# Moving the low weight buffers of three weight streams by 128 bytes in SBUF

## What is computed

```python
h = rms_norm(x)
q, kc, vc, ks, vs, kw, vw, gn, u, v, ga, gb = split(h @ w_in)          # 1024 x 4376
o_a = nsa_attention(q, ...)            # compressed + selected + window branches
o_b = u * gmlp_spatial(v)
x += (sigmoid(ga) * (o_a @ w_branch_a) + sigmoid(gb) * (o_b @ w_branch_b)) @ w_out
x += cross_attention(rms_norm(x) @ w_cq, memory) @ w_co
h = rms_norm(x)
x += (silu(h @ w_gate) * (h @ w_up)) @ w_down                           # 1024 x 2816, 2816 x 1024
y = rms_norm(x)
```

## Time and profile before

| | |
|---|---|
| device time, median of 3 runs | 2215.38 us (2214.71 to 2215.53) |
| the profiled execution | span 2214.8 us from the first to the last instruction |
| TensorE matmul busy | 2118.7 us, 96% |
| VectorE / GpSimd / ScalarE busy | 929.5 / 611.8 / 551.1 us |
| mean share of the DMA engines | 22.7% of their time for the largest queue |
| mean granted TensorE clock | 0.983 of 2.4 GHz |

### The profile page before, as it was taken

One profiled execution on the slowest core, in us unless ns is written; L12 is line 12 of the kernel. 1 busy time (PEld: TensorE's weight loads), 2 busy tenths in 40 slices (PEclk: granted clock), 3 DMA queues, 4 the chain that ended last, 5 costly groups with the idle time before them and its releaser, 6 DMA issues. The chain is left out here.

```text
span 2214.8 us, 38450 instructions
## 1 busy us (share of the span) xinstructions
PE 2118.7 (96%) x14076; PEld 1962.7 (89%) x14076; DVE 929.5 (42%) x1958; ACT 551.1 (25%) x1151; POOL 611.8 (28%) x531
## 2 busy tenths in 40 slices
PE   7999999988989999799999988999999999999998
PEld 6999999965855767599999878999999999999997
DVE  4111111186336676455661346563333333333335
ACT  5002211122326655222030332221111111111112
POOL 2233322245224444412212322212212122121220
PEclk9999999999979999899999999999999999999999
DMA  6212222394323000544212432110211112111121
GB/s 199 55 47 62 72 90 93 127 262 151 90 62 136 1 2 1 142 146 146 85 39 67 191 120 62 46 49 29 67 31 55 48 33 62 33 53 48 33 62 78
DMA packets 206648, 175.77 MB, mean 79 GB/s; under 512 B 25867, under 2 KB 186348, under 8 KB 205963
## 3 DMA queue, kind: packets, MB, share of 16 engines
q1 hardware_dynamic: 197450, 152.96, 22.7%
q10 hardware_dynamic: 4448, 11.81, 1.5%
q0 software_dynamic: 4640, 9.61, 1.5%
HBM read 147.02 MB, written 27.39 MB: 79 GB/s over the span
## 5 line engine op out<-in xcount | busy, mean ns | idle before, releaser
L152 POOL TENSOR_TENSOR tail_w_lo<-mem_last_slot,tail_w_hi 128x1024 fp32r<-128x1024 f32 (+1 forms) x94 | 183.3, 1950 | 689.8 <-ACT tail_w_hi L140 689.8
L191 PE MATMUL ff_psum<-tail_hi,tail_w_hi 128*128 128x352 f32 x1056 | 341.2, 323 | 1.0 <-PEq L2112 1.0
L192 PE MATMUL ff_psum<-tail_lo,tail_w_hi 128*128 128x352 f32 x1056 | 338.5, 321 | 0.0
L193 PE MATMUL ff_psum<-tail_hi,tail_w_lo 128*128 128x352 f32 x1056 | 338.2, 320 | 0.0
L191 PE MATMUL bank<-mix_hi,in_w_hi 128*128 128x352 f32 x840 | 271.9, 324 | 1.3 <-issue 1.3
L192 PE MATMUL bank<-mix_lo,in_w_hi 128*128 128x352 f32 x840 | 270.0, 321 | 0.0
L193 PE MATMUL bank<-mix_hi,in_w_lo 128*128 128x352 f32 x840 | 269.9, 321 | 0.0
L140 ACT CAST tail_w_hi<-mem_last_slot 128x1024 fp32r<-128x1024 f32 (+1 forms) x94 | 81.2, 863 | 509.3 <-PE ff_psum L193 433.4
L191 PEld LDWEIGHTS ff_psum<-tail_hi,tail_w_hi 128*128 128x128 f32 x1056 | 198.1, 188 | 2.0 <-issue 1.5
L192 PEld LDWEIGHTS ff_psum<-tail_lo,tail_w_hi 128*128 128x128 f32 x1056 | 198.4, 188 | 0.1
L193 PEld LDWEIGHTS ff_psum<-tail_hi,tail_w_lo 128*128 128x128 f32 x1056 | 197.9, 187 | 0.0
(11 more groups left out here) (394 smaller groups left out, 3822.2 us busy)
## 6 DMA issues: line engine op xcount, KB each, us to landing
in_raw<-w_in SPq DMA_DIRECT2D x70, 256.0 KB, 3.2
mem_last_slot<-w_gate SPq DMA_DIRECT2D x44, 256.0 KB, 3.2
mem_last_slot<-w_up SPq DMA_DIRECT2D x44, 256.0 KB, 3.3
mem_last_slot<-w_down SPq DMA_DIRECT2D x80, 128.0 KB, 2.2
gate_kept<-x_first ACTq DMA_DIRECT2D x16, 528.0 KB, 2.7
uv<-gate_kept SPq DMA_DIRECT2D x16, 528.0 KB, 4.6
mem_ring<-cache_mem_v SPq DMA_DIRECT2D x8, 1024.0 KB, 13.2
mem_ring<-cache_mem_k SPq DMA_DIRECT2D x7, 1024.0 KB, 7.0
```

What stands on the lines that cost most here:

```text
L152: pool.tensor_tensor(lo, raw, hi.bitcast(F32), ALU.subtract).then_inc(self.split, 1)
L191: pe.matmul(out, hi, x_hi, start=k == 0, stop=False)
L192: pe.matmul(out, hi, x_lo, start=False, stop=False)
L193: last = pe.matmul(out, lo, x_hi, start=False, stop=k == len(terms) - 1)
```

## The change

`place_halves` allocates each low buffer 256 bytes longer and uses its middle, so that the low weights start 128 bytes after the start of their allocation. Nothing else is edited.

```diff
+W_SHIFT = 32
 ...
     def place_halves(self, sb, ctx, name, depth, slots=(0, 1)):
         for s in slots:
             self.w_hi[s] = sb(ctx, f"{name}_w_hi{s}", [P, depth, P], F32R)
-            self.w_lo[s] = sb(ctx, f"{name}_w_lo{s}", [P, depth, P], F32R)
+            self.w_lo[s] = sb(ctx, f"{name}_w_lo{s}", [P, depth * P + 2 * W_SHIFT], F32R)[:, W_SHIFT:W_SHIFT + depth * P].rearrange("p (k c) -> p k c", k=depth)
```

## The result

| | before | changed |
|---|---|---|
| device time, median of 8 runs each | 2215.82 us | 2221.79 us (2219.78 to 2225.68) |
| ratio | | 1.0024, 95% interval 1.0014 to 1.0035 |
| span of the profiled execution | 2214.8 us | 2219.4 us |

The changed kernel is slower by 0.24%, some 5.3 us. That lies in the range, between the forecast (no change) and the slower rival, and just beyond the 0.2% that a measurement can tell. All ratios are of undisturbed executions: one of the kernel before (5344 us) and one of both128 (11060 us) lie far outside the others and are left out.

What follows compares the result with a forecast made beforehand. The prediction took TensorE's own products as the bound. Every part of the change was put at 0 us, so the profiled 2214.8 us plus 0.6 for the median gave 2215.4 us, with a range of 2204 to 2230.

Steps and rivals of the forecast that it cites:

- slower rival: Own streams' matmuls: each flip of relative place costs cycles; 14.7 us at full size (2230), put at 2227; chance 0.30.
- What bounds the kernel: TensorE, busy for 96% of the span; its weight products, 1501 us or 68%, are what the change can touch.
- No cost on GpSimd, ScalarE and SyncE: They handle the same sizes elsewhere; GpSimd has 689.8 us of waiting to cover a slower subtraction: 0 us.
- No cost of the moves by 256 and 512 bytes: High weights of slot 1 and activations of mid and tail keep their relative place modulo 256: 0 us.
- Only relative places count: TensorE's gaps follow where weights and activations start against each other modulo 256, not their absolute places; no size.
- The swap: Own streams, gap after line 192: 161.7 and 155.0 ns exchange between even and odd k + c; sum 0.
- The down projection: Low weights there: 1.4 ns to either side on 1440 matmuls, 2.0 us, taken as 0.
- The faster rival: Own streams: the low load under the second product is cheap in all steps; -8.9 us, 2206.5; chance 0.27.
- The far case: Own streams: all matmuls at the shortest averaged gap, 155.0 ns; -31.6 us, 2184; chance 0.03.
- The rule against any effect: TensorE has independent read ports for moving operand and weights and never waits, so the kernel stays at 2215.4 us.

Runs made afterwards that it cites:

- both128: Kernel before, with high and low weights of all streams both moved 128 bytes against the activations; measured ratio 0.9999.
- nolow: Changed kernel, with the third matmul of each step reading high weights in place of low ones; one run, 2217.3 beside 2217.4 us.
- low256: Kernel before, with low weights moved by 256 bytes against the high weights of slot 0, in place of 128; measured ratio 1.0000.
- align64: Kernel before, with 8 floats ahead of the big buffers on either side, so all start at multiples of 64 bytes; measured ratio 0.9987.
- actlow128: Kernel before, with the low activations of all streams starting 128 bytes later and weights as before; measured ratio 1.0097.
- high128: Kernel before, with the high weights moved by 128 bytes and the low weights kept in place modulo 256; measured ratio 1.0027.
- stride_in: Kernel before, with the weight blocks of a tile 640 bytes apart in place of 512, in the stream in alone; measured ratio 1.0029.
- both64: Kernel before, with high and low weights both moved 64 bytes against the activations; measured ratio 1.0045.
- both32: Kernel before, with high and low weights both moved 32 bytes against the activations; measured ratio 1.0068.

## Why the prediction was right or wrong

- **What bounds the kernel.** Right. The change is in the gaps of TensorE's weight products, on all dense own tiles, and the waits of the other engines didn't move.
- **No cost on GpSimd, ScalarE and SyncE.** Right, and shown by nolow: the writes to the new place are there and cost nothing.
- **No cost of the moves by 256 and 512 bytes.** Right, by low256.
- **Only relative places count.** Right as against absolute places, by low256 and align64, where buffers are elsewhere and own tiles take the same. But they are not all that counts: in actlow128 the same places gave 11.480 and 11.640 us.
- **The swap.** This is the step that failed. The prediction had the gap after line 192 follow the place of the block being loaded under it, and the two values 161.7 and 155.0 change places. They stayed: 161.7 and 155.8 after. Since both128 and high128 do exchange even and odd, and the change doesn't, the low block's own place doesn't choose between them; the high blocks' place does. The sum in a running chunk is nevertheless what the swap gave, 0, by another course: chunk 0 takes 3.813 before and after. The forecast of no change was lost on a term that the prediction put at nothing without naming it: what happens when a new chunk begins. Chunks 1 and 2 have some steps off the pattern there, before as well (the gaps of chunk 1 begin with 189, 194, 186 and 195, 192, 192 cycles). With low and high weights apart more steps are off, up to the fifth, and they are dearer, 0.047 us per tile in all, 5.2 us in the kernel. Which chunk starts are disturbed agrees with what the addresses say: k + c is odd in the last step of chunk 0 and again in the first of chunk 1, even in the last of chunk 1 and again in the first of chunk 2, and goes on alternating only from chunk 2 into chunk 0 of the next tile, the one chunk that begins in the pattern.
- **The size.** That the measured time lies in the range is in part luck: the range was wide enough for it only because it held the slower rival at full size. That rival's 11.3 to 14.7 us were twice to three times too much, and its mechanism is refuted: the place flips at each matmul in the steady part of the changed kernel, at no extra cost, and stride_in, without flips, is slower.
- **The down projection.** Its sum stayed within the 2 us allowed (0 in the steady tiles, 0.1 us in the first ones of the five groups), though single gaps changed there, too.
- **The faster rival** has nothing for it in any run: where the second product's gap was short in every step (chunk 1 of stride_in), the third's was longer, and no steady own tile was cheaper than before.
- **The far case.** The 149.2 ns that the prediction set beside it are, in the section of the Trainium skill that it names, the gap of an isolated matmul, and not that of a stream in which each matmul has a weight load of its own, as here. No tile came nearer to it than 158.98 ns per matmul.
- **The rule against any effect.** The Trainium skill, "SBUF — State Buffer", section "Who interferes with whom", has two independent read ports for TensorE and TensorE waiting on no one. On the waiting, nolow agrees: GpSimd's writes to the new place cost TensorE nothing. But own tiles took 11.447 to 11.667 us with the same instructions and the granted clock at 1.00, and it made a difference where weights lay against activations (both64, both32). So independent ports don't mean that places can't matter: for these float32r products they moved a tile by up to 1.9%, and the measurement decides.

What stays open is the cause inside TensorE or SBUF. It is shown that the places of weights and activations against each other change the time, and that a move of weights by 256 bytes doesn't. Why it takes up to five steps to come back into the pattern, and what makes a chunk dear for a given distance, is not shown, and no run here takes one of the two reads away.

## What to carry to other kernels

Where TensorE runs without idle time and both its operands are 4 bytes wide, as here (no other width was run), compare the time between starts of equal matmuls in two streams, or in one stream from step to step: if they differ with no wait and a full clock, the buffers' places against each other may matter; in this kernel they were worth 0.4% to 1.9% of a tile, and a pad of 32 to 128 bytes ahead of one buffer tries it at no cost in instructions. Keep all operand pairs at the same distance (here 0 or 128 bytes modulo 256 with high and low alike); in the tiles of 72 matmuls, moving one of a set that is used in turn was worse each of the four times it was tried, while in the down projection it cost nothing twice. Sum such an effect from the time of whole repeats of the pattern, the beginnings included, and not from the steady middle.

## What the runs showed that was not expected

- The times of steady tiles don't vary freely. Own tiles took 11446.7, 11480.0, 11493.3, 11520.0, 11533.3, 11560.0, 11566.7, 11640.0 and 11666.7 ns, and down tiles 5726.7, 5773.3, 5786.7 and 5826.7. All these differ by whole multiples of 6.67 ns (5, 7, 11, 13, 17, 18, 29 and 33 of them for own tiles, counted from the first), while averaged single gaps differ by as little as 0.83 ns. 6.67 ns is 8 of the cycles of 0.833 ns used above. Tiles that don't yet repeat are off this grid, such as the first dense tile of the stream in before, 11468 ns.
- Two patterns of gaps can run at the same places. In that first dense tile, all of chunk 0 runs in gaps of 159, 161, 162 and 159, 158, 161 ns and takes 3.840 us; in a later tile of the same slot it takes 3.813, in the pattern of the earlier trace rows. The change of chunk ended the dearer pattern. In the changed kernel, the first tile behind each down projection takes 11.529 us in place of 11.493.
- The sign of a distance counts: weights 32 bytes above and 32 below the activations' place modulo 128 gave 11.667 and 11.520 us.
- Even the best arrangement found is 158.98 ns for a matmul of 352 columns, and no run had an own tile below 11.4467 us, though every kernel has single gaps of about 155 ns somewhere.
